# One decoder layer on one core: the samples' SSD states are read in the recurrent steps and updated in a second pass in the output steps

## The chip, the cores and the metric

The kernel runs on one core of one Trainium2 chip. The metric is the device time of one launch in microseconds. The engines are TensorE (PE, matmuls; PEld is its weight load), VectorE (DVE), ScalarE (ACT), GpSimd (POOL) and SyncE (SP). Each works through its own list of instructions in order and waits on semaphores that the others raise. ACT and SP also issue DMAs.

## What is computed

One layer of a hybrid decoder for one prompt of 256 tokens and 8 samples of one token each, D_MODEL 2048: a SwiGLU, a mixer with an RG-LRU group and a Mamba-2 SSD group side by side, a second SwiGLU, and a final norm. All is float32. What the change touches is the SSD recurrence of the 8 samples. With sequences of one token, the reference's scan comes to this for each sample and head (state 64 x 128):

```python
# ssd_scan with T = 1, for each sample b and head h
new_state = exp(dt * A) * old_state + outer(x * dt, B)   # stored as ssm_sample
y         = new_state @ C                                # + D * x, then gate and norm
# and so also
y         = exp(dt * A) * (old_state @ C) + (x * dt) * (B . C)
```

The last line is algebra, not a line of the reference. There are 16 heads in 2 groups; B and C (128 numbers) are those of the group. The state of all samples and heads is 4.2 MB, read once and written once.

## The kernel before, in words

PE's work is the weight matmuls. Weights come through SP's DMAs into `raw`, ACT copies each piece to `w_hi` (L686), rounded to the matmul's type, DVE makes `w_lo` = raw - w_hi (L1006), and PE multiplies hi x hi, lo x hi and hi x lo (L1648 to L1650). `w_hi` and `w_lo` have four buffers, so ACT may be three pieces ahead of PE. The program runs in steps of 8 pieces (24 matmuls a piece), each step in four slots j = 0 to 3; `u` = 4t + j counts slots of a kind of step. In every slot each engine does its part for two pieces and then its tasks (`act_tasks`, `dve_tasks`, `pe_tasks`), so the order on each engine is written out in the code.

Between the first SwiGLU and the second stand: 3 xbc steps and the dt step, 4 recurrent steps ("lru", u = 0 to 15), 2 z steps (u = 0 to 7), 4 output steps ("out", u = 0 to 15). The recurrent steps hold the RG-LRU with its convolutions (`conv_half`: L1205 twice, L1212, L1214 for each tile; the last one raises `conv_ready`) and its gate matmuls (`gates`, L1813 and L1814, which wait for `conv_ready`), the prompt's SSD products (`bcast`, `y_item`), and the samples' states.

The samples' states are 16 items of 128 x 512 (two heads' rows by four samples by 128 numbers). POOL does four tensor products or sums for each (`sample_item`): state times decay (L643), B times x dt (L647), their sum, which is the new state (L649), and new state times C (L652); DVE sums that over the 128 numbers (`sum_item`, L1287). B and C spread over the partitions come by `col_rows` on PE (8 matmuls into bank b7) and a copy by ACT (`spread_copy`, L817), one of each for every four items. ACT issues the load of each item (L806) and the store of its new state (L811) in the recurrent steps; four buffers `state` take turns.

In the last z slot (u = 7) DVE finishes `y_item` 15 (L1281, raises `y_placed` to 16), then the gate of the last two tiles (L1410 to L1419), the samples' y (L1424 to L1428, raises `sumsq_ready`), three w_lo, the reciprocal of the norm (L1433), and, tile by tile, L1436 and h_lo (L1440). PE has put `y_placed` and the sum over partitions (L1614, `sumsq_total`) after two pieces of the first output step. The output steps are weight pieces on PE, w_hi on ACT, and w_lo with `add_branch` (L1127 to L1138) on DVE. In slot 2 ACT copies the small output rows and issues eleven output DMAs (L924, L926). POOL has nothing after L661.

## Time and profile before

| | |
|---|---|
| median of 3 runs | 2179.3 us (2177.04 to 2180.01) |
| the profiled execution | 2176.04 us, span 2174.3 us |
| PE busy | 2119.3 us, 97% of the span |
| DVE busy | 1205.4 us, 55% |
| ACT busy | 859.6 us, 40% |
| POOL busy | 123.5 us, 6% |
| DMA | 534.17 MB, mean 246 GB/s |

Times in the trace count from the start of the span. The recurrent steps lie from about 1037 to 1180 us, the z steps to about 1230, the output steps to about 1327. A row of the timeline gives start, duration, engine, line, operation, what is written and read, and in brackets how long the engine was idle before, and who ended that. Two rows of one engine can overlap by some tenths of a microsecond, since an instruction starts while the one before it drains. Line numbers are those of the kernel before.

### The profile page before, as it was taken

Reading aid. Unit: us, or ns where it says so; the run is one execution under the profiler, and the core shown is the slowest. Engines: PE = TensorE matmul, PEld = TensorE weight load, DVE = VectorE, ACT = ScalarE, POOL = GpSimd, SP = SyncE. Lnnn points to the kernel's source line nnn. Section 1 sums busy time; section 2 is a strip of 40 time slices with the busy share of each in tenths; the row PEclk is TensorE's granted clock in tenths of the full one; section 3 lists DMA queues with packets and bytes.
Section 4 is the critical chain, followed back from the end, with each engine's and each line's share of the span. In section 5 each row is a group of like instructions: output and inputs, shape, how many; then the busy total and the mean of one; then the engine's idle time right before and its main releaser. Section 6 shows DMA issues by size and latency. Waiting matters only on the chain.

```text
span 2174.3 us, 40038 instructions
## 1 busy us (share of the span) xinstructions
PE 2119.3 (97%) x17437; PEld 1978.0 (91%) x17437; DVE 1205.4 (55%) x1649; ACT 859.6 (40%) x1058; POOL 123.5 (6%) x148
## 2 busy tenths in 40 slices
PE   6999999999999999999999999999999999999998
PEld 4988989988888889989988998999998999999998
DVE  4355576444444445577789967444444444445555
ACT  3433333333333333356655534333333333333332
POOL 0000000000000000011674000000000000000000
PEclk9999999999999999999999999999999999999999
DMA  9988886899888877647555485765667886755453
GB/s 357 344 300 293 286 279 245 279 337 367 304 307 309 308 277 258 239 147 222 161 172 161 156 281 205 263 236 173 228 235 254 306 277 237 248 169 171 146 175 117
DMA packets 394269, 534.17 MB, mean 246 GB/s; under 512 B 13031, under 2 KB 357999, under 8 KB 375407
## 3 DMA queue, kind: packets, MB, share of 16 engines
q1 hardware_dynamic: 371792, 519.28, 69.5%
q10 hardware_dynamic: 22303, 12.33, 2.0%
q8 instruction: 138, 2.26, 0.4%
q14 instruction: 36, 0.29, 0.0%
HBM read 524.37 MB, written 7.19 MB: 244 GB/s over the span
## 4 chain that ended last, share of the span: by engine, by line
PE 90%; DVE 6%; ACT 1%; issue 1%; SPq 1%; DMA 1%; ACTq 0%; DVEq 0%
PE main L1648 24%; PE main L1649 23%; PE main L1650 23%; PE b L1571 5%; PE main L1714 4%; PE main L1716 3%; PE main L1715 3%; DVE w_lo L1006 2%; PE b L1581 1%; ACT w_hi L686 1%; SPq L530 1%; PE b L1594 1%; DVE ntile L1099 1%; DMA first<-in_w_ada 1%; DVE h_lo L1104 1%
## 5 line engine op out<-in xcount | busy, mean ns | idle before, releaser
L1006 DVE TENSOR_TENSOR w_lo<-raw,w_hi 128x1024 fp32r<-128x1024 f32 (+2 forms) x720 | 791.3, 1106 | 868.3 <-ACT w_hi L686 866.9
L686 ACT ACTIVATE w_hi<-raw 128x1024 fp32r<-128x1024 f32 (+2 forms) x720 | 685.6, 956 | 1068.0 <-PE main L1650 908.5
L1648 PE MATMUL main<-h_hi,w_hi 128*128 128x264 f32 x2960 | 851.3, 288 | 11.6 <-DVE h_lo L1112 3.9
L1649 PE MATMUL main<-h_lo,w_hi 128*128 128x264 f32 x2960 | 843.6, 285 | 0.0
L1650 PE MATMUL main<-h_hi,w_lo 128*128 128x264 f32 x2960 | 842.3, 285 | 0.0
L1648 PEld LDWEIGHTS main<-h_hi,w_hi 128*128 128x128 f32 x2960 | 559.3, 189 | 31.8 <-DVE w_lo L1006 20.4
L1649 PEld LDWEIGHTS main<-h_lo,w_hi 128*128 128x128 f32 x2960 | 557.9, 188 | 0.4
L1650 PEld LDWEIGHTS main<-h_hi,w_lo 128*128 128x128 f32 x2960 | 557.7, 188 | 0.0
L1648 PE MATMUL main<-act_hi,w_hi 128*128 128x264 f32 x1408 | 402.1, 286 | 0.0
L1650 PE MATMUL main<-act_hi,w_lo 128*128 128x264 f32 x1408 | 400.4, 284 | 0.0
L1649 PE MATMUL main<-act_lo,w_hi 128*128 128x264 f32 x1408 | 399.8, 284 | 0.0
L1648 PEld LDWEIGHTS main<-act_hi,w_hi 128*128 128x128 f32 x1408 | 264.6, 188 | 10.1 <-issue 9.2
L1649 PEld LDWEIGHTS main<-act_lo,w_hi 128*128 128x128 f32 x1408 | 265.3, 188 | 0.0
L1650 PEld LDWEIGHTS main<-act_hi,w_lo 128*128 128x128 f32 x1408 | 264.6, 188 | 0.0
L1714 PE MATMUL main<-h_hi,w_hi 128*128 128x264 f32 x704 | 205.2, 292 | 9.1 <-DVE w_lo L1006 4.7
L1716 PE MATMUL main<-h_hi,w_lo 128*128 128x264 f32 x704 | 200.8, 285 | 0.0
L1715 PE MATMUL main<-h_lo,w_hi 128*128 128x264 f32 x704 | 200.8, 285 | 0.0
L1714 PEld LDWEIGHTS main<-h_hi,w_hi 128*128 128x128 f32 x704 | 133.8, 190 | 23.5 <-issue 18.6
L1715 PEld LDWEIGHTS main<-h_lo,w_hi 128*128 128x128 f32 x704 | 134.2, 191 | 0.0
L1716 PEld LDWEIGHTS main<-h_hi,w_lo 128*128 128x128 f32 x704 | 133.6, 190 | 0.0
L1571 PE MATMUL b<-ada,cT 128*32 128x512 f32 x1024 | 116.9, 595 | 0.0
L1571 PEld LDWEIGHTS b<-ada,cT 128*32 128x32 f32 x1024 | 29.8, 109 | 61.9 <-issue 57.6
(277 smaller groups left out, 1002.6 us busy)
## 6 DMA issues: line engine op xcount, KB each, us to landing
raw<-in_w_up SPq DMA_DIRECT2D x132, 1024.0 KB, 5.2
ada<-in_w_ada SPq DMA_DIRECT2D x112, 1024.0 KB, 8.6
raw<-in_w_down SPq DMA_DIRECT2D x96, 768.0 KB, 5.1
raw<-in_w_up SPq DMA_DIRECT2D x88, 512.0 KB, 5.3
raw<-in_w_in SPq DMA_DIRECT2D x36, 1024.0 KB, 5.4
ada<-in_w_ada_f SPq DMA_DIRECT2D x32, 1024.0 KB, 10.1
ada<-in_w_ada SPq DMA_DIRECT2D x56, 512.0 KB, 7.7
raw<-in_w_down SPq DMA_DIRECT2D x32, 512.0 KB, 4.3
```

Of the source, the lines that this page charges most:

```text
L530: sp.dma_start(quarter_slot(i)[:, v], quarter_columns(0, i, v)).then_inc((ada_landed, first_landed)[i // 4][i % 4], 16)
L686: A(split_view(w_hi, m, kind), raw_piece(m, kind), ACT.Copy).then_inc(hi_done, 1)
L1006: TT(split_view(w_lo, m, kind), raw_piece(m, kind), split_view(w_hi, m, kind).bitcast(F32), ALU.subtract).then_inc(lo_done, 1)
L1099: STT(ntile[:, k % 4, :], x[:, k, 0:NT], gain[:, k, 0:1], rstd[:, 0:NT], ALU.mult, ALU.mult).then_inc(aff_ready, 1)
L1104: return STT(h_lo[:, k, 0:NT], ntile[:, k % 4, :], mods[:, shift, k, 0:1], h_hi[:, k, 0:NT].bitcast(F32), ALU.add, ALU.subtract)
L1571: last = MM(b4[32 * j:32 * j + 32, :], cT[:, k, :], ada[:, k % 4, j * 512:(j + 1) * 512], start=k == 0, stop=k == KD - 1, tile_position=(0 ...
L1648: MM(out, wh, hi[:, k, :], start=k == 0, stop=False)
L1649: MM(out, wh, lo[:, k, :], start=False, stop=False)
L1650: last = MM(out, wl, hi[:, k, :], start=False, stop=k == total - 1)
L1714: MM(out, wh, h_hi[:, k, :], start=kk == 0, stop=False)
L1715: MM(out, wh, h_lo[:, k, :], start=False, stop=False)
L1716: last = MM(out, wl, h_hi[:, k, :], start=False, stop=kk == 3)
```

## The change

The states go through in two passes. In the recurrent steps POOL makes one product for each item, old state times C (`sample_read`), and DVE sums it as before; nothing is stored. In slot 1 of the z steps DVE multiplies the sums by the decay and adds x dt times (B . C); the products of B and C are made by DVE in recurrent slot 0 (`bc`) and summed over partitions by one matmul in z slot 0. In slot 3 of the z steps ACT loads the first four items a second time (`state_again`). POOL makes the new states (`sample_step`: state times decay, B times x dt, sum) after `y_placed` 16. ACT stores them and loads the other twelve items in output slots 1 to 12; each of these loads waits for the store from the same buffer. C is spread in recurrent slots j = 0 (four `col_rows` instead of eight there), B in z slots 1 to 4, into the space of `gates_w`, which is free by then; POOL's product of B goes to the space of `s0t`. The number of `col_rows` and copies stays eight.

```diff
-            def sample_item(n):
+            def sample_read(n):
...
-                ch.link(pool.tensor_tensor(st, st, dcs_f[:, t, bs].unsqueeze(2).to_broadcast([P, 4, NSTATE]), ALU.mult))
-                pool.wait_ge(spread_done, 2 * q + 1)
+                pool.wait_ge(spread_done, q + 1)
                 if n >= 2:
                     pool.wait_ge(st_sum, n - 1)
-                ch.link(pool.tensor_tensor(pr, spread_b[:, :, :],
+                pool.tensor_tensor(prod[n % 2], state[:, i, :, :], spread_c[:, :, :], ALU.mult).then_inc(st_prod, 1)
+
+            def sample_step(n):
+
+                (q, i), t, bs = (n // 4, n % 4), *item_place(n)
+                st, pr = state[:, i, :, :], outer[:, n % 2, :, :]
+                pool.wait_ge(st_in[i], 16 * (4 + q + 1))
+                ch.link(pool.tensor_tensor(st, st, dcs_f[:, t, bs].unsqueeze(2).to_broadcast([P, 4, NSTATE]), ALU.mult))
+                pool.wait_ge(spread_done, 4 + q + 1)
+                ch.link(pool.tensor_tensor(pr, spread_b[:, q, :, :],
                                            xsdt[:, t, bs].unsqueeze(2).to_broadcast([P, 4, NSTATE]), ALU.mult))
                 pool.tensor_tensor(st, st, pr, ALU.add).then_inc(st_new, 1)
...
             capture_h(3)
+            pool.wait_ge(y_placed, 16)
+            for n in range(16):
+                sample_step(n)
...
+            def state_again(n):
+
+                t, bs = item_place(n)
+                if n < 4:
+                    act.wait_ge(st_prod, 13 + n)
+                else:
                     act.wait_ge(st_out[n % 4], 16 * (n // 4))
...
                         state_load(r + 1)
-                    if 2 <= r <= 17:
-                        state_store(r - 2)
+                    if r == 19:
+                        for n in range(4):
+                            state_again(n)
...
-                if kind == "lru" and j < 2:
-                    spread_copy(2 * t + j, (spread_b, spread_c)[j][:, :, :])
+                if kind == "lru" and j == 0:
+                    spread_copy(t, spread_c[:, :, :])
+                if kind == "z" and 1 <= u <= 4:
+                    spread_copy(3 + u, spread_b[:, u - 1, :, :])
...
                 if kind == "out":
+                    for n in range(16):
+                        if u == 1 + 3 * n // 4:
+                            state_store(n)
+                    for n in range(4, 16):
+                        if u == 2 + 3 * (n - 4) // 4:
+                            state_again(n)
...
+                        TT(bc[:, :, :], xbc[:, 8:10, NT:COLS], xbc[:, 10:12, NT:COLS], ALU.mult).then_inc(bc_product, 1)
...
+                if kind == "z" and u == 1:
+                    dve.wait_ge(st_sum, 16)
+                    TT(samp[:, 0:KW, :], samp[:, 0:KW, :], dcs_f[:, :, :], ALU.mult)
+                    dve.wait_ge(bc_summed, 1)
+                    sums = b4[:, 0:2 * NB].rearrange("p (g b) -> p g b", g=2)
+                    for g in range(2):
+                        ins_ = TT(ybc[:, 4 * g:4 * g + 4, :], xsdt[:, 4 * g:4 * g + 4, :],
+                                  sums[:, g:g + 1, :].to_broadcast([P, 4, NB]), ALU.mult)
+                    ch.link(ins_)
+                    ch.link(TT(samp[:, 0:KW, :], samp[:, 0:KW, :], ybc[:, :, :], ALU.add))
...
+                if kind == "z" and u == 0:
+                    pe.wait_ge(bc_product, 1)
+                    pe.wait_ge(gate_taken, 16)
+                    MM(b4[:, 0:2 * NB], ones[:, :], bc[:, :, :].rearrange("p g b -> p (g b)"),
+                       start=True, stop=True).then_inc(bc_summed, 1)
+                if kind == "z" and 1 <= u <= 4:
+                    col_rows(3 + u)
```

How the order moves, at the two places that matter. First POOL, at items 14 and 15 of the recurrent steps and its end, before:

```order
L643 TENSOR_TENSOR state<-state,dcs_f 128x512
L647 TENSOR_TENSOR ntile<-spread_b,xsdt 128x512
L649 TENSOR_TENSOR state<-state,ntile 128x512
L652 TENSOR_TENSOR ntile<-state,spread_c 128x512
L643 TENSOR_TENSOR state<-state,dcs_f 128x512
L647 TENSOR_TENSOR part<-spread_b,xsdt 128x512
L649 TENSOR_TENSOR state<-state,part 128x512
L652 TENSOR_TENSOR part<-state,spread_c 128x512
L657 COPY outcol<-rec 128x2
L661 COPY outcol<-rec 128x2x8
```

And after (line numbers of the changed kernel; `ntile` and `part` are the two product buffers, `gates_w` now holds the spread B, `s0t` its product):

```order
L648 TENSOR_TENSOR ntile<-state,spread_c 128x512 [waits st_sum,spread_done,st_in2]
L648 TENSOR_TENSOR part<-state,spread_c 128x512 [waits st_sum,spread_done,st_in3]
L664 COPY outcol<-rec 128x2 [waits hl_ready]
L668 COPY outcol<-rec 128x2x8
L655 TENSOR_TENSOR state<-state,dcs_f 128x512 [waits st_in0,y_placed]
L657 TENSOR_TENSOR s0t<-gates_w,xsdt 128x512 [waits spread_done,pool_chain]
L659 TENSOR_TENSOR state<-state,s0t 128x512 [waits pool_chain]
L655 TENSOR_TENSOR state<-state,dcs_f 128x512 [waits st_in1]
L657 TENSOR_TENSOR s0t<-gates_w,xsdt 128x512 [waits spread_done,pool_chain]
L659 TENSOR_TENSOR state<-state,s0t 128x512 [waits pool_chain]
```

Six of eight products leave this place, and 48 of them stand behind `y_placed` 16, at the end of POOL's list. Second ACT's list, from the second norm's last tile to the first pieces of the second output step, before (L686 is w_hi, L912 the norm's h_hi; the output DMAs in the middle are the same in both, and end with `out_ssm_prompt`):

```order
L912 ACTIVATE h_hi<-xbc 128x264 [waits aff_ready]
L686 ACTIVATE w_hi<-raw 128x1024 [waits piece_used,w_landed0]
L918 ACTIVATE xdt<-b 128x512 [waits out_turned]
L919 ACTIVATE xdt<-b 128x128
L924 DMA out_lru_conv_prompt<-xdt 24x128 [waits out_rows_ready]
```

And after:

```order
L933 ACTIVATE h_hi<-xbc 128x264 [waits aff_ready]
L829 DMA out_ssm_sample<-state 128x4x128 [waits st_new] x2
L696 ACTIVATE w_hi<-raw 128x1024 [waits piece_used,w_landed0]
L829 DMA out_ssm_sample<-state 128x4x128 [waits st_new]
L824 DMA state<-in_state_ssm 128x4x128 [waits st_out0]
L824 DMA state<-in_state_ssm 128x4x128 [waits st_out1]
L945 ACTIVATE xdt<-b 128x512 [waits out_turned]
L946 ACTIVATE xdt<-b 128x128
L951 DMA out_lru_conv_prompt<-xdt 24x128 [waits out_rows_ready]
```

Three stores and two loads have come in, and the loads wait for stores issued just ahead of them (`st_out0`, `st_out1`).

## Rows read from the trace of the kernel before

**Rows 1.** The page: busy time, share of the span, instructions

```profile
PE 2119.3 (97%) x17437; PEld 1978.0 (91%) x17437; DVE 1205.4 (55%) x1649; ACT 859.6 (40%) x1058; POOL 123.5 (6%) x148
```

**Rows 2.** Stretches: length, busy time by engine, granted clock, DMA share, GB/s

```profile
core 0: us, PE busy (x) PEld busy (x) DVE busy (x) ACT busy (x) POOL busy (x), PEclk, DMA share, GB/s
1037.00:1180.00 143.00, 133.37 (x1037) 127.25 (x1036) 122.03 (x138) 83.48 (x128) 105.40 (x92) 0.98 0.55 166
...
1260.00:1327.00 67.00, 67.00 (x549) 67.00 (x548) 42.84 (x59) 24.39 (x23) 0.00 (x0) 1.00 0.75 256
```

**Rows 3.** Timeline of PE: every idle time in the recurrent steps

```profile
1089.78 0.78 PE L1813 MATMUL b<-cval,gates_w 128*128 128x264 f32 x1 [2.43 <-issue]
...
1125.72 0.68 PE L1813 MATMUL b<-cval,gates_w 128*128 128x264 f32 x2 [1.55 <-issue]
...
1135.39 0.68 PE L1813 MATMUL b<-cval,gates_w 128*128 128x264 f32 x2 [1.26 <-issue]
...
1160.58 0.68 PE L1813 MATMUL b<-cval,gates_w 128*128 128x264 f32 x2 [0.92 <-issue]
...
1169.33 0.68 PE L1765 MATMUL b<-tri,dA 128*128 128x128 f32 x4 [1.79 <-DVE s L1372]
...
1171.68 0.78 PE L1813 MATMUL b<-cval,gates_w 128*128 128x264 f32 x1 [1.68 <-issue]
```

**Rows 4.** Timeline of DVE ahead of the first idle time, POOL working

```profile
1084.62 2.50 DVE L1205 SCALAR_TENSOR_TENSOR cfull<-cin,small,cfull 128x288 f32<-128x288 f32 x2
1087.16 1.37 DVE L1212 SCALAR_TENSOR_TENSOR cval<-cin,small,cfull 128x256 f32<-128x256 f32 x1
1088.46 1.23 DVE L1214 SCALAR_TENSOR_TENSOR cval<-cin,small,cfull 128x8 f32<-128x8 f32 x1
```

**Rows 5.** Timeline of DVE, the same instructions a slot later, POOL idle

```profile
1093.68 1.13 DVE L1205 SCALAR_TENSOR_TENSOR cfull<-cin,small,cfull 128x288 f32<-128x288 f32 x2
1094.84 0.49 DVE L1212 SCALAR_TENSOR_TENSOR cval<-cin,small,cfull 128x256 f32<-128x256 f32 x1
1095.24 0.23 DVE L1214 SCALAR_TENSOR_TENSOR cval<-cin,small,cfull 128x8 f32<-128x8 f32 x1
```

**Rows 6.** Timeline of POOL beside rows 4, one item's first three products

```profile
1084.37 1.23 POOL L643 TENSOR_TENSOR state<-state,dcs_f 128x512 f32<-128x512 f32 x1
1085.68 1.14 POOL L647 TENSOR_TENSOR part<-spread_b,xsdt 128x512 f32<-128x512 f32 x1
1086.89 1.36 POOL L649 TENSOR_TENSOR state<-state,part 128x512 f32<-128x512 f32 x1
```

**Rows 7.** DVE: two w_lo beside POOL; L1281's duration min/median/max in ns

```profile
1161.64 3.99 DVE L1006 TENSOR_TENSOR w_lo<-raw,w_hi 128x1024 fp32r<-128x1024 f32 x2
...
L1281 DVE SCALAR_TENSOR_TENSOR xbc<-xbc,dfeat,b x16: 334/339/348, 1083.2 to 1231.1; 128x128 f32<-128x128 f32 x16
```

**Rows 8.** Timeline of DVE in the last z slot, up to the w_lo

```profile
1232.20 0.68 DVE L1416 SCALAR_TENSOR_TENSOR xbc<-xbc,silu_g 128x512 f32<-128x512 f32 x1
...
1234.37 0.22 DVE L1424 TENSOR_TENSOR xbc<-xbc,dfeat 128x64 f32<-128x64 f32 x1
...
1235.61 3.48 DVE L1006 TENSOR_TENSOR w_lo<-raw,w_hi 128x1024 fp32r<-128x1024 f32 x3
```

**Rows 9.** Timeline of PE in the output steps

```profile
1236.11 0.60 PE L1614 MATMUL b<-sumsq,ones 128*128 128x264 f32 x2
...
1250.45 0.39 PE L1648 MATMUL main<-h_hi,w_hi 128*128 128x264 f32 x1 [0.93 <-DVE h_lo L1440]
...
1260.04 0.28 PE L1648 MATMUL main<-h_hi,w_hi 128*128 128x264 f32 x1
```

**Rows 10.** Timeline of ACT around the output DMAs

```profile
1249.01 1.04 ACT L686 ACTIVATE w_hi<-raw 128x1024 fp32r<-128x1024 f32 x1
...
1255.81 2.01 ACT L686 ACTIVATE w_hi<-raw 128x1024 fp32r<-128x1024 f32 x2 [5.11 <-issue]
```

**Rows 11.** The stores of new states: ns to issue, us to landing

```profile
L811 ACTq DMA_DIRECT2D out_ssm_sample<-state x16: 378/520/893, 1050.3 to 1185.6; - x16
...
DMA to landing us min/median/max: 2.3/4.2/5.8
```

**Rows 12.** Timeline of DVE, the w_lo behind the output DMAs

```profile
1256.97 1.23 DVE L1006 TENSOR_TENSOR w_lo<-raw,w_hi 128x1024 fp32r<-128x1024 f32 x1 [2.20 <-ACT w_hi L686]
```

More of the change, by code:

```diff
@@ L210, in build @@
             ("shift_row", [P, D], F32), ("yrows", [P, 2, D], F32), ("ysrow", [P, P], F32)])
-        (xbc, out_l, cin, cfull, cval, xdt, xdec, btok, cbm, s0, s0t, state, spread_b, spread_c,
+        (xbc, out_l, cin, cfull, cval, xdt, xdec, btok, cbm, s0, s0t, state, spread_c,
          gates_w, th, rec, dA, spt, sp2, sp3, sp4, lam2, half_b, exp_a, cst, decl, tot, cdf, dfeat,
-         dts_f, dcs_f, xsdt, zs, later, ncs) = layout([
+         dts_f, dcs_f, xsdt, zs, later, ncs, bc, ybc) = layout([
             ("xbc", [P, KX, COLS], F32),
@@ L229, in build @@
             ("dts_f", [P, KW, NB], F32), ("dcs_f", [P, KW, NB], F32), ("xsdt", [P, KW, NB], F32),
-            ("zs", [P, KW, NB], F32), ("later", [P, P], F32), ("ncs", [P, NHEAD], F32)])
+            ("zs", [P, KW, NB], F32), ("later", [P, P], F32), ("ncs", [P, NHEAD], F32), ("bc", [P, 2, NB], F32), ("ybc", [P, KW, NB], F32)])
         prod_even = (ntile[:, 2:4, :].rearrange("p a n -> p (a n)")
@@ L234, in build @@
         gel, aa = silu_g, part
+        spread_b = gates_w.rearrange("p a t n -> p (a t n)").rearrange("p (q b n) -> p q b n", q=4, b=4)
+        outer = s0t.rearrange("p (a b n) -> p a b n", a=2, b=4)
         dtq = part2[:, 0, :]
@@ L283, in build @@
         st_new, st_prod, st_sum = sem("st_new"), sem("st_prod"), sem("st_sum")
+        bc_product, bc_summed = sem("bc_product"), sem("bc_summed")
         z_tanh, sz_ready = sem("z_tanh"), sem("sz_ready")
@@ L664, in _ @@
             for n in range(16):
-                sample_item(n)
+                sample_read(n)
                 if n % 4 == 1:
@@ L814, in spread_copy @@
                 act.wait_ge(col_spread, n + 1)
-                if n >= 2:
-                    act.wait_ge(st_prod, 4 * (n // 2))
+                if 1 <= n < 4:
+                    act.wait_ge(st_prod, 4 * n)
                 A(dst.rearrange("p b n -> p (b n)"), b7[:, :], ACT.Copy).then_inc(spread_done, 1)
@@ L1786, in col_rows @@
             def col_rows(n):
-                q, cc = n // 2, n % 2
+                is_b, q = n // 4, n % 4
                 g, half = q // 2, q % 2
@@ L1793, in col_rows @@
                     pe.wait_ge(spread_done, n)
-                if n % 2 == 0 and n:
-                    pe.wait_ge(gate_taken, 2 * n)
+                    pe.wait_ge(gate_taken, 16 if is_b else 4 * n)
                 for i in range(4):
                     col = NT + 4 * half + i
-                    last = MM(b7[:, i * P:(i + 1) * P], xbc[:, 8 + 2 * cc + g, col:col + 1].to_broadcast([P, P]),
+                    last = MM(b7[:, i * P:(i + 1) * P], xbc[:, (8 if is_b else 10) + g, col:col + 1].to_broadcast([P, P]),
                               ident[:, :], start=True, stop=True)
@@ L1807, in gates @@
                 if t % 2 == 0:
-                    pe.wait_ge(spread_done, t + 2)
+                    pe.wait_ge(spread_done, t // 2 + 1)
                 if t == 0:
@@ L1854, in pe_tasks @@
                 if kind == "lru":
-                    if j < 2:
-                        col_rows(2 * t + j)
-                    else:
+                    if j == 0:
+                        col_rows(t)
+                    if j >= 2:
                         gates(2 * t + j - 2)
+                if kind == "z" and u == 0:
[5 more added lines that the diff above has]
+                    col_rows(3 + u)
                 if kind == "out" and u == 1:
```

9 lines of the change are left out of this document (3 added, 6 removed).

## Prediction, written before the changed kernel ran

> **What bounds the kernel now.** First the page's busy shares: TensorE (PE) is busy 97% of the span [rows 1], so a change pays only where it removes idle PE time, or adds it. Then the stretches: in the recurrent steps (1037 to 1180 us) PE is busy 133.37 of 143 us, while VectorE (DVE) is busy 122.03 and GpSimd (POOL) 105.40; in the output steps from 1260 on PE is busy without a gap and DVE 42.84 of 67 us [rows 2]. Third, PE's idle times inside the recurrent steps: 2.43, 1.55, 1.26, 0.92, 1.79 and 1.68 us, **9.63 us** in all [rows 3]. Five stand before L1813, the gate matmul, which waits for `conv_ready`. The trace calls the releaser "issue", but DVE's L1214, whose end raises `conv_ready`, runs from 1088.46 for 1.23 us and so ends at 1089.69 [rows 4], and PE starts at 1089.78 [rows 3]. The sixth (1169.33) waits for DVE's work on `s0`. So DVE is late there, and PE waits for it.
>
> Why is DVE late? The same instructions stand twice in its rows. With POOL idle, L1205 (two of them) takes 1.13 us, L1212 0.49, L1214 0.23 [rows 5]; ten microseconds earlier, with POOL's products running end to end [rows 6], 2.50, 1.37 and 1.23 [rows 4]. That is 0.69, 0.88 and 1.00 us more for each instruction, 3.25 us in four of them; w_lo (L1006) took 3.99 us for two where 1.23 is its free time [rows 7, 12], 0.77 us more each. Each of these reads two tensors in SBUF. L1281, which has one operand in PSUM, never took over 0.35 us in 16 instructions [rows 7]. DVE loses **0.7 to 1.0 us to each POOL product that meets such an instruction**, and three products last from 1084.37 to 1088.25, 3.9 us a sample item [rows 6].
>
> This is what the Trainium skill says (SBUF — State Buffer, "Who interferes with whom"): a DVE instruction with two SBUF inputs contends with a GpSimd instruction that reads SBUF. By that rule, the trace agrees in kind; its stronger half comes below as a rival.
>
> **The change, part by part.**
>
> 1. *Recurrent steps, less POOL work.* Each of 16 items goes from four products to one, so 48 of 64 go. Before the first stall the four contended instructions alone lost 3.25 us, more than the 2.43 us that PE waited [rows 3 to 5]; with one product an item a hit or so of 0.7 to 1.0 us remains, and L1006 and the scans further up lose less too. The waits for POOL's sums and ACT's waits for new states go as well. What is late next would be ACT's convolution start, which I see no sign of. PE's clock belongs here: the granted mean is 0.98 over 143 us [rows 2], about 2.9 us lost to stretches at the lower level (1.2 instead of 2.4 GHz), which come with the longer idle times (L1813 takes 0.78 us at 1089.78 and at 1171.68, 0.68 as a pair elsewhere [rows 3]). Bounds: each of the six idle times shrinks by one missed hit of 0.7 us, 4 us; and all goes, 9.63 + 2.9 = 12.5. I take **-12.0**, near the upper end, because the stretch (3.25 us in four instructions) exceeds every single idle time.
>
> 2. *Moved column rows and the B.C product.* Four `col_rows` with their copies go from the recurrent to the z steps: as many matmuls as before, zero net. One small matmul and some six small DVE products are new; L1424, as wide, takes 0.22 us [rows 8]. In the z steps DVE gains the time of the moved matmuls, and POOL is silent. Taken at zero; uncovered 1.3 us.
>
> 3. *The first four items of the second pass meet the second norm.* POOL now waits for `y_placed` 16, the end of DVE's L1281 in the last z slot, and its states have been loaded. From there DVE makes the chain that PE waits for: gate, squares, sample sum, then w_lo, reciprocal, and the eight parts of h. There is no slack in it: `sumsq` is done when L1006 starts at 1235.61 and PE asks for it at 1236.11, and the last h_lo already costs 0.93 us at 1250.45 [rows 8, 9]. POOL's 12 products need 12 x 1.3 = 16 us [rows 6], the same stretch. DVE has ten instructions with two SBUF inputs in its first 8 us: three like L1416 (0.8 each, between L1205's 0.69 and L1212's 0.88), four like L1424 (1.00 each, L1214's loss), three w_lo (0.8): 2.4 + 4.0 + 2.4 = **+8.8**. Bounds: half the products meet nothing, 5; all twelve cost 0.9, 11.
>
> 4. *Stores and loads on ACT's queue.* Ahead of its w_hi for the second piece of the second output step ACT now issues three stores and two loads, and each load waits for the store of its buffer to land. A store takes 0.52 us to issue and lands after 4.2 (2.3 to 5.8) [rows 11]. The second load cannot go before 0.52 + 4.2 = 4.7 us, plus about 0.4 for its issue, 5.1, of which 1.04 is the w_hi that stood there before [rows 10]: 4.1 us more. Before, w_hi started at 1255.81 (after the output DMAs), its w_lo ended at 1256.97 + 1.23 = 1258.20, and PE took that piece at 1260.04 [rows 9, 10, 12]: 1.84 us of cover. So 2.3 us, and 0.4 for a product that may meet the w_lo: **+2.7** (0.5 to 5). Queued behind these waits are only ACT's own w_hi; later ones have three pieces of lead.
>
> 5. *The other twelve items in the output steps.* 36 products; if each met a DVE instruction at 0.8 us, 28.8 us more for DVE, which is idle 67 - 42.84 = 24.2 us there [rows 2], some 21 of them while POOL runs: 8 us short. If only every second one does, 14.4, it fits. The lead is zero at the start (part 4), so lumps count; I take **+4.0** (0 to 8).
>
> 6. *Clock.* PE idles for over 5 us at once in part 3. One stretch at the lower level costs half of the 2.9 us of two: **+1.4** (0 to 3).
>
> Not priced: 4.2 MB read a second time, since the output steps move 256 GB/s [rows 2], and the page's first slice 357.
>
> Sum: -12.0 + 8.8 + 2.7 + 4.0 + 1.4 = **+4.9 us**. The profiled run took 2176.04 us (span 2174.3), the median of the runs is 2179.3, 3.3 above; the profiled one would become 2180.9, and on the median I forecast 2184.2.
>
> **The rivals.**
>
> *Faster: POOL gives way.* POOL's products in the second pass could be the ones that wait, and DVE's chain loses only 4 us; w_lo is served in time (+1), no clock stretch: -12 + 4 + 1 = -7, 2172. For it: only 12 products lie on the chain. Against: in rows 4 and 6 POOL kept 1.14 to 1.36 us a product while DVE's small instruction took five times its time. It decides if L1424 to L1427's successors take under 0.5 us.
>
> *Much slower: the output steps do not fit both engines.* If a product shuts DVE out for all of its 1.14 to 1.36 us, 36 of them hold some 45 us. Beside them stand at least the w_lo, one for each of the 549 / 24 = 23 pieces in the 67 us, 28 us, and at most all of DVE's 43 [rows 2]: 6 to 21 us too many for 67, say 14 instead of 4. Then -12 + 8.8 + 2.7 + 14 + 1.4 = +15, 2194. Against it: L1205 grew by 0.69 us only, beside products of 1.14 and more [rows 4 to 6], so they overlap in part. The Trainium skill (SBUF — State Buffer, the same section) has this rule: whoever issues first holds the port for the whole instruction and the other fully blocks.
>
> *The stalls stay.* The change may not free PE in the recurrent steps, because the single products still hit the convolutions or ACT is next: gain 4 instead of 12, so +13, 2192. For it: DVE is at 85% there [rows 2]. Against: it would have to be late without most of its losses.
>
> **How the numbers follow.** Forecast 45% (its own range 2178 to 2191), POOL gives way 20%, does not fit 12%, stalls stay 13%, and 10% for mixtures on either side. The range takes in the first rival and nearly the second: 2170 to 2198. A measurement of this kernel tells about 0.2%, 4.4 us, from no change. Faster by more: the first rival and a few of the mixtures, 24%. Slower by more: the two slow rivals and 26 points of the forecast's 45, which lies just over the line, 51%. Within: 25%.
>
> **What would show it.** Right if L1813's idle times are gone, and if PE instead waits over 5 us for the `sumsq` matmul of the first output step, behind DVE instructions of 0.2 us stretched to over 1 us; then 2 to 3 us at the second piece of the next step, behind w_lo; then small waits for w_lo while POOL works. Wrong if PE meets the norm without waiting (faster), if the waits for w_lo add up to more than 8 us (much slower), or if L1813 still waits (stalls stay). The forecast itself falls if the new waits of the output steps sum to under 8 or over 25 us.

## The result, and the profile after

The changed kernel takes 2182.65 us (median of 20 runs, 2179.69 to 2186.46), the kernel before 2177.78 us (20 runs, 2175.93 to 2180.07). The ratio is 1.0022 with a 95% interval of 1.0016 to 1.0028: **4.9 us slower**, and slower beyond doubt, though only just above the 0.2% line of the prediction. The profiled execution has a span of 2180.9 us where the one before had 2174.3.

Four stretches of the changed kernel, in the columns of [rows 2] (length, busy time of PE, of its weight loads, of DVE, ACT and POOL, granted clock, DMA share, GB/s): the recurrent steps, the z steps, the norm, and most of the output steps.

```profile
1024.00:1167.00 143.00, 143.00 (x1147) 137.75 (x1146) 107.07 (x165) 93.54 (x139) 48.92 (x50) 1.00 0.49 155
1167.00:1219.00 52.00, 51.24 (x438) 48.86 (x437) 46.31 (x88) 31.19 (x50) 0.33 (x2) 1.00 0.53 163
1218.00:1250.00 32.00, 25.19 (x178) 23.94 (x179) 30.80 (x42) 11.61 (x19) 17.20 (x12) 0.89 0.47 144
1250.00:1318.00 68.00, 61.31 (x481) 60.25 (x479) 54.11 (x50) 20.25 (x20) 58.24 (x36) 0.97 0.96 313
```

In the recurrent steps PE now works all 143 us at a clock of 1.00; before it was 133.37 of 143 at 0.98 [rows 2]. All six idle times of [rows 3] are gone. The price stands in the last two lines, where before PE had only the two short waits for h_lo ahead of 1260 and none behind it [rows 2, 9]. PE's own timeline names each new wait in its last bracket (start, duration, line, then the idle time ahead of it and what ended it):

```profile
1228.88 1.22 PE L1652 MATMUL b<-sumsq,ones 128*128 128x264 f32 x2 [4.89 <-DVE sumsq L1466]
...
1246.18 0.39 PE L1686 MATMUL main<-h_hi,w_hi 128*128 128x264 f32 x1 [0.91 <-DVE h_lo L1478]
...
1257.59 0.39 PE L1686 MATMUL main<-h_hi,w_hi 128*128 128x264 f32 x1 [1.68 <-DVE w_lo L1033]
...
1265.84 0.39 PE L1686 MATMUL main<-h_hi,w_hi 128*128 128x264 f32 x1 [2.11 <-DVE w_lo L1033]
...
1295.81 0.39 PE L1686 MATMUL main<-h_hi,w_hi 128*128 128x264 f32 x1 [0.31 <-DVE w_lo L1033]
...
1304.32 0.39 PE L1686 MATMUL main<-h_hi,w_hi 128*128 128x264 f32 x1 [2.38 <-DVE w_lo L1033]
...
1319.64 0.39 PE L1686 MATMUL main<-h_hi,w_hi 128*128 128x264 f32 x1 [1.84 <-DVE w_lo L1033]
```

L1652 is the `sumsq` matmul of [rows 9], L1686 the main matmul there. The 0.91 us for h_lo was there before (0.93), and two shorter ones ahead of it, 0.18 and 0.83 us, stand where 0.56 stood. The rest is new: 4.89 us at the norm, 1.68 at the second piece of the second output step, and then 2.11, 0.31, 2.38 and 1.84, together **6.64 us**, for w_lo. The timeline of DVE shows what stands behind the 4.89 us, the successors of [rows 8]:

```profile
1222.33 1.67 DVE L1457 TENSOR_TENSOR sumsq<-sumsq,part 128x512 f32<-128x512 f32 x1
1224.03 0.94 DVE L1462 TENSOR_TENSOR xbc<-xbc,dfeat 128x64 f32<-128x64 f32 x1
1225.01 1.08 DVE L1463 TENSOR_TENSOR xbc<-xbc,samp 128x64 f32<-128x64 f32 x1
1226.13 1.30 DVE L1464 SCALAR_TENSOR_TENSOR xbc<-xbc,zs 128x64 f32<-128x64 f32 x1
1227.47 0.96 DVE L1465 TENSOR_TENSOR samp<-xbc 128x64 f32<-128x64 f32 x1
1228.46 0.27 DVE L1466 TENSOR_REDUCE sumsq<-samp 128x8 f32<-128x64 f32 x1
1228.65 6.09 DVE L1033 TENSOR_TENSOR w_lo<-raw,w_hi 128x1024 fp32r<-128x1024 f32 x3
```

Four products of 64 columns, 0.22 us before, take 0.94 to 1.30 us. Three w_lo take 6.09 us where they took 3.48 [rows 8]. L1466, which reads one tensor, keeps 0.27 us. POOL's timeline beside the four small products shows how the two engines share:

```profile
1223.40 1.50 POOL L655 TENSOR_TENSOR state<-state,dcs_f 128x512 f32<-128x512 f32 x1
1224.97 1.04 POOL L657 TENSOR_TENSOR s0t<-gates_w,xsdt 128x512 f32<-128x512 f32 x1
1226.09 1.26 POOL L659 TENSOR_TENSOR state<-state,s0t 128x512 f32<-128x512 f32 x1
1227.31 1.04 POOL L655 TENSOR_TENSOR state<-state,dcs_f 128x512 f32<-128x512 f32 x1
```

They take turns, a whole instruction at a time. POOL's products end at 1224.90, 1226.01, 1227.35 and 1228.35, and each of DVE's four small ones ends 0.07 to 0.08 us later: it has waited for nearly the whole product. The long ones do the same. In the second pass 21 w_lo are lengthened, and every one of them ends 1.08 us after a POOL product has ended, where a w_lo that meets nothing takes 1.22; POOL's products beside w_lo end 0.90 us (L655, L657) or 1.13 to 1.15 (L659) after the w_lo has ended, where they take 1.04 and 1.26 when they meet nothing. So all but 0.11 to 0.14 us of an instruction stands behind the whole of the other engine's. The one that comes first keeps its time: L1454 starts at 1220.17 and takes 0.68 us as before the change [rows 8], and POOL's product that starts at 1220.30 takes 1.45.

In the output steps four w_lo in a row take 8.14 us, 2.03 each, and POOL's products, in turns with them, as much as 2.15:

```profile
1263.84 8.14 DVE L1033 TENSOR_TENSOR w_lo<-raw,w_hi 128x1024 fp32r<-128x1024 f32 x4
```

```profile
1264.79 2.15 POOL L659 TENSOR_TENSOR state<-state,s0t 128x512 f32<-128x512 f32 x1
1266.90 2.02 POOL L655 TENSOR_TENSOR state<-state,dcs_f 128x512 f32<-128x512 f32 x1
1269.00 1.90 POOL L657 TENSOR_TENSOR s0t<-gates_w,xsdt 128x512 f32<-128x512 f32 x1
1270.97 2.15 POOL L659 TENSOR_TENSOR state<-state,s0t 128x512 f32<-128x512 f32 x1
```

An item then takes 6.2 us (L659 to L659), where the stores stand four in three slots of two pieces, a piece being 2.93 us of PE: one each 4.4 us. ACT's timeline, with the instructions that issue transfers as ACTq, shows what follows. L829 is the store of new states, L696 w_hi:

```profile
1277.96 1.06 ACT L696 ACTIVATE w_hi<-raw 128x1024 fp32r<-128x1024 f32 x1 [1.87 <-PE main L1688]
1278.54 6.58 ACTq L829 DMA_DIRECT2D out_ssm_sample<-state  x2
1285.16 0.52 ACTq L824 DMA_DIRECT2D state<-in_state_ssm  x1
1285.78 2.01 ACT L696 ACTIVATE w_hi<-raw 128x1024 fp32r<-128x1024 f32 x2 [6.75 <-issue]
```

Two stores hold ACT for 6.58 us instead of about 1, because the new state they store isn't made; ACT is idle for 6.75 us before the w_hi behind them, and DVE's w_lo comes after that. This stand by itself costs PE little: DVE is idle for 0.73 us, and PE's next wait is 0.31 us, ten microseconds on. But in the second pass ACT is idle for 3 to 8 us between two w_hi seven times, DVE is idle for w_hi 3.93 and 3.31 us more, and then makes w_lo of 2 us each. The waits of 2.38 and 1.84 us come after some 10 us in which DVE was never idle. The queue and the lengthened w_lo make them together.

Where the time went, read by following one instruction of each place through both traces: the last z slot's y item starts 12.28 us earlier than before; the last h_lo, 18.84 us behind it before, is now 26.92 us behind (+8.08); the second piece of the second output step is then 2.45 us early (1257.59 against 1260.04), so another +1.8; the first norm wait of the feed-forward steps behind is 6.75 us late, so +9.2 from there on.

### The profile page after: what moved, and what is told of

Its sections match the earlier page's. It is cut to its first block, busy times and chain, and to the rows that moved or that the text cites. A ratio compares the mean times of both kernels' runs of the same rounds, so it can differ in the third digit from the quotient of the medians.

```text
span 2180.9 us, 40054 instructions
## 1 busy us (share of the span) xinstructions
PE 2123.3 (97%) x17439; PEld 1982.3 (91%) x17439; DVE 1208.4 (55%) x1654; ACT 858.8 (39%) x1058; POOL 139.0 (6%) x148
## 4 chain that ended last, share of the span: by engine, by line
PE 84%; DVE 6%; POOL 3%; issue 3%; ACT 1%; DMA 1%; SPq 1%; ACTq 0%; DVEq 0%; POOLq 0%
PE main L1686 22%; PE main L1687 22%; PE main L1688 22%; PE b L1609 5%; PE main L1752 4%; PE main L1754 3%; PE main L1753 3%; DVE w_lo L1033 2%; POOL state L659 1%; PE b L1619 1%; POOL state L655 1%; POOL s0t L657 1%; ACT w_hi L696 1%; SPq L533 1%; PE b L1632 1%
## 5 line engine op out<-in xcount | busy, mean ns | idle before, releaser
L1033 DVE TENSOR_TENSOR w_lo<-raw,w_hi 128x1024 fp32r<-128x1024 f32 (+2 forms) x720 | 805.9, 1128 | 874.0 <-ACT w_hi L696 872.7
L696 ACT ACTIVATE w_hi<-raw 128x1024 fp32r<-128x1024 f32 (+2 forms) x720 | 684.6, 956 | 1078.4 <-PE main L1688 887.7
L1686 PE MATMUL main<-h_hi,w_hi 128*128 128x264 f32 x2960 | 853.8, 288 | 19.3 <-DVE w_lo L1033 11.6
L1686 PEld LDWEIGHTS main<-h_hi,w_hi 128*128 128x128 f32 x2960 | 562.3, 190 | 40.3 <-DVE w_lo L1033 30.9
L1686 PE MATMUL main<-act_hi,w_hi 128*128 128x264 f32 x1408 | 402.1, 286 | 0.0
L1686 PEld LDWEIGHTS main<-act_hi,w_hi 128*128 128x128 f32 x1408 | 264.7, 188 | 10.1 <-issue 9.2
```

Of the source, the lines that this page charges most:

```text
L696: A(split_view(w_hi, m, kind), raw_piece(m, kind), ACT.Copy).then_inc(hi_done, 1)
L1033: TT(split_view(w_lo, m, kind), raw_piece(m, kind), split_view(w_hi, m, kind).bitcast(F32), ALU.subtract).then_inc(lo_done, 1)
L1686: MM(out, wh, hi[:, k, :], start=k == 0, stop=False)
```

## The experiments

All ratios are against the kernel before, run beside each experiment on the same chip; 0.001 is 2.2 us. The intervals reach 0.0009 to 0.0016 to either side, so two experiments that lie less than about 0.0015 apart are not told from each other. Line numbers in rows are those of each kernel.

**The first term alone.** The kernel before, with three of an item's four products taken out: the new states are left out, the old ones are stored.

```
-  ch.link(pool.tensor_tensor(st, st, dcs_f[...], ALU.mult))
...
-  ch.link(pool.tensor_tensor(pr, spread_b[...], xsdt[...], ALU.mult))
-  pool.tensor_tensor(st, st, pr, ALU.add).then_inc(st_new, 1)
+  pool.memset(pr[:, 0, 0:1], 0.0).then_inc(st_new, 1)
```

> The kernel before, with three of the four products of each sample item taken out (they are one memset of a single column, so the new states are left out and the old ones are stored); the recurrent steps keep their loads, stores and waits, nothing is added behind them. It measures the first term of the sum by itself. Theory (POOL's products that read SBUF are what makes DVE late): the six idle times of PE before L1813 and the state update go, 9.6 us and some 2 to 3 us of clock, so 11 to 13 us below before, 2164 to 2166 us. Rival (the gain came from the queues and waits that the change took out of the recurrent steps, not from the products): those are all still there, so at most 4 us below, 2172 or more.

Measured: 2164.44 us, ratio 0.9940 (0.9926 to 0.9953), 13.1 us less. The stretch of the recurrent steps has no idle PE time:

```profile
1024.00:1167.00 143.00, 143.00 (x1150) 137.91 (x1151) 108.89 (x164) 93.00 (x140) 44.60 (x66) 1.00 0.59 181
```

The rival falls: stores, loads and waits are all still there. The gain is that DVE meets fewer products: 13.1 us, where the trace of the change has 12.28.

**The change without its second products.** The states are loaded a second time, waited for and stored; the 48 products are left out, and so are the new states.

```
+  pool.memset(pr[:, 0, 0:1], 0.0).then_inc(st_new, 1)
+  pool.wait_ge(st_new, n + 1)
+  return
```

> The changed kernel with all 48 second-pass products left out (one column is written instead, so new states are left out); the second loads, the stores and all waits between them stay. This prices what the DMAs and their waits on ACT's queue cost alone. Theory A: the loss in norm and output steps (some 19 us in the traces) was nearly all products; what stays is the wait of 1 to 2 us at the second piece of the second output step, so 2182.7 - 17 = 2164 to 2168 us. Rival D (the second load of 4.2 MB and ACT's queue are the cost): at least 6 us of the output steps' loss stays, 2171 us or more.

Measured: 2165.58 us, ratio 0.9948 (0.9932 to 0.9963). That is 16 us under the change. It is 1.7 us above the last experiment by the ratios, which is within the noise of the two (nothing to some 6 us): that is what the second reading, the moved matmuls and the extra issues on ACT's queue cost together. Nearly all that the change loses comes with the products of the second pass.

**Products that only write.** The 48 products replaced by as many memsets of 1344 columns; the new states are left out.

```
+  fill = gates_w.rearrange("p a t n -> p (a t n)")[:, 0:1344]
+  ch.link(pool.memset(fill, 0.0))
+  ch.link(pool.memset(fill, 0.0))
+  pool.memset(fill, 0.0).then_inc(st_new, 1)
```

> The changed kernel, but each of the 48 second-pass products is replaced by a POOL memset of 1344 columns, about 1.2 us long, that reads nothing; the new states are left out. POOL is as busy as before, or nearly. Theory A in its narrow form (a DVE instruction with two SBUF inputs is held up by POOL instructions that READ SBUF): no DVE instruction is stretched, no wait at the sumsq matmul, no w_lo waits beyond the one that stands behind ACT's DMA issues; 2165 to 2170 us. Rival C (any POOL work of that length holds DVE up, or what costs is POOL being busy so that ACT waits for its stores): DVE stretched as before, 2178 to 2183 us. If only ACT's waits matter, items are done in 3.6 us and the time lies between.

Measured: 2173.76 us, ratio 0.9982 (0.9973 to 0.9991), between what the two theories had, which the expectation names as the third outcome. POOL's timeline and DVE's at the place of the four small products:

```profile
1222.19 1.22 POOL L658 MEMSET gates_w<- 128x1344 f32 x1
1223.47 1.23 POOL L659 MEMSET gates_w<- 128x1344 f32 x1
1224.76 1.22 POOL L657 MEMSET gates_w<- 128x1344 f32 x1
1226.03 1.22 POOL L658 MEMSET gates_w<- 128x1344 f32 x1
```

```profile
1223.76 0.23 DVE L1469 TENSOR_TENSOR xbc<-xbc,dfeat 128x64 f32<-128x64 f32 x1
1224.02 0.23 DVE L1470 TENSOR_TENSOR xbc<-xbc,samp 128x64 f32<-128x64 f32 x1
...
1225.00 3.48 DVE L1040 TENSOR_TENSOR w_lo<-raw,w_hi 128x1024 fp32r<-128x1024 f32 x3
```

POOL works end to end there, and DVE's products keep 0.23 us and its three w_lo 3.48, as before the change. So it isn't POOL's being busy that costs: it is POOL's *reading* from SBUF while DVE reads two tensors there. The kernel is still some 7 us slower than the one without products. Its PE waits for w_lo, 0.99, 2.50 and 0.80 us, come after DVE was idle for w_hi (5.19, 7.29 and 2.72 us), while its w_lo kept 1.22 us, so ACT's waits in the stores and loads cost by themselves. Here POOL was late because the states were: a load issued at 1259.14 us landed 16.1 us later.

**Only the first four items left out.** These are the ones that meet the norm; their new states are left out.

```
+  if n < 4:
+      pool.wait_ge(spread_done, 4 + q + 1)
+      pool.memset(pr[:, 0, 0:1], 0.0).then_inc(st_new, 1)
+      pool.wait_ge(st_new, n + 1)
+      return
```

> The changed kernel, but for the first four items of the second pass POOL makes one write of one column instead of its three products, so the new states of these four items are left out; loads, stores and all waits stay. Theory A: the norm chain on DVE returns to its 18.8 us from 26.9, PE's wait before the sumsq matmul goes, time 2182.7 - 8 = 2174 to 2176 us. Rival B (chain late for another reason): wait of 4.9 us stays, time within 2 us of 2182.7.

Measured: 2175.70 us, ratio 0.9992 (0.9983 to 1.0001), 6.5 us under the change. PE meets `sumsq` without waiting, and the waits for h_lo are those of the kernel before:

```profile
1237.81 0.39 PE L1691 MATMUL main<-h_hi,w_hi 128*128 128x264 f32 x1 [0.57 <-DVE h_lo L1483]
1240.48 0.39 PE L1691 MATMUL main<-h_hi,w_hi 128*128 128x264 f32 x1 [0.93 <-DVE h_lo L1483]
```

Behind them the waits for w_lo are 1.75, 0.61, 0.62, 2.39, 0.79 and 2.13 us, 8.3 us, as in the change (8.3 with its 1.68). The norm term of the sum, 8.1 us in the trace, comes back: 6.5 us, which the noise does not tell from 8.1.

**The second pass after the norm.** Everything is computed; POOL starts when the last h_lo is made, and stores and loads stand two slots later.

```
-  pool.wait_ge(y_placed, 16)
+  pool.wait_ge(h_ready, 3 * KD)
...
-  if u == 1 + 3 * n // 4:            # stores
+  if u == 3 + 3 * n // 4:
...
-  if u == 2 + 3 * (n - 4) // 4:      # loads
+  if u == 4 + 3 * (n - 4) // 4:
```

> The changed kernel, whole, but POOL starts the second pass only when the last h_lo of the second norm is made (it waits for h_ready instead of y_placed), and ACT's stores and later loads come two slots later. Theory A (POOL's products stretch DVE's two-input instructions wherever they meet): PE's 4.9 us wait before the sumsq matmul goes, and the 8 us by which DVE's norm chain was longer with it; the w_lo wait of 1.7 us at the second piece of the second output step goes too. The 48 products then share 12 slots with w_lo instead of 36, so the waits for w_lo in the output steps stay or grow by 1 to 3 us. Time 8 to 10 us below the changed kernel's 2182.7, some 2173 to 2176, that is 0 to 2 % of a percent range around -0.1 to -0.2 % against the kernel before. Rival B (the norm chain is late for another reason, for example the DVE work moved into the z steps): the 4.9 us wait stays and the time is within 2 us of the changed kernel's.

Measured: 2180.48 us, ratio 1.0012 (1.0003 to 1.0021). The norm is free again, but the time did not come back: a miss. The 2.2 us under the change are within the noise. The stretch from 1250 to 1335 us and the group of main matmuls from 1250 to 1330, with its idle time on the right:

```profile
1250.00:1335.00 85.00, 73.86 (x550) 71.02 (x550) 67.88 (x62) 23.94 (x24) 65.35 (x41) 0.94 0.89 288
```

```profile
L1686 PE MATMUL main<-h_hi,w_hi 128*128 128x264 f32 x175 | 52.2, 298 | 11.0 <-DVE w_lo L1033 11.0
```

11.0 us of waits for w_lo instead of 8.3 (6.64 and 1.68), and a clock of 0.94. 48 products at up to 2 us each, with items that wait for their loads, fill what is left of the output steps, and two stores again hold ACT for 4.9 to 5.5 us. Moving the products off the norm trades one wait for another.

**Eight buffers.** The second four lie in `th` and `xdec`, which are free by then, so that no load waits for a store just issued. The stores stand a slot later. The loads move the other way: items 4 to 7 are loaded ahead of the row DMAs, and the second eight two slots earlier than in the change.

```
+  more = [v[:, 0:1024]... for v in (th..., xdec)]
...
-  act.wait_ge(st_out[n % 4], 16 * (n // 4))
+  if count:
+      act.wait_ge(gone, count)       # only from item 8 on
```

> The whole change with eight buffers for the states of the second pass instead of four (the second four lie in buffers of the recurrence that are free by then), so that no load waits for a store that has just been issued, and the stores stand a slot later. The same 48 products start at the same time, beside the second norm. If ACT's blocking in the stores and loads is what makes w_hi and so w_lo late in the output steps (theory: some 4 to 5 of the 6.6 us of waits there), this is 4 to 6 us below the change, 2176 to 2179 us, and the waits for w_lo there sum to under 2.5 us. If contention of POOL and DVE makes w_lo late by itself (rival), the sum of the waits stays at 5 us or more and the time within 2 us of the change's 2182. The waits of the norm (4.9 us before the sumsq matmul) stay in both.

Measured: 2181.41 us, ratio 1.0014 (1.0005 to 1.0023). The waits for w_lo did fall as that theory has it:

```profile
L1712 PE MATMUL main<-h_hi,w_hi 128*128 128x264 f32 x193 | 55.4, 287 | 3.3 <-DVE w_lo L1058 2.6 <-DVE h_lo L1503 0.7
```

2.6 us in the 75 us from 1250 on, a little over the 2.5 of the theory; the changed kernel has 8.3 there. The median w_lo takes 2.00 us there, against 2.06, so lengthened w_lo alone do not make those waits: with w_hi on time most of them are covered. How much of the 5.7 us is ACT's queue stays open, since POOL also has 30 products left in this stretch instead of 36. And the time fell by 1.7 us only, which is within the noise. The stretch of the norm shows why:

```profile
1218.00:1250.00 32.00, 23.19 (x150) 21.80 (x150) 31.34 (x33) 10.37 (x17) 24.47 (x18) 0.84 0.32 99
```

POOL has 24.47 us of work there instead of 17.20. In the changed kernel it paused for items 4 and 5, whose buffers were not free, and that pause spared the eight parts of h. Without it PE waits 0.75, 1.56, 1.61 and 0.66 us for h_lo, 4.6 us where the change has 0.83 and 0.91, and the clock falls to 0.84. The gain went into a new wait.

**Eight buffers and the late start.** Both edits together, stores and loads one slot later again.

> The same eight buffers, and POOL starts the second pass only when the second norm has been made (as in e1_late), with stores and loads a slot later again. POOL then has some 89 us for 16 items of 4.3 (free) to 6 us (beside DVE). Theory (ACT's blocking is the larger part of the waits in the output steps, contention the smaller): the norm costs nothing and the waits sum to under 4 us: 2169 to 2173 us. Rival (contention alone makes w_lo late, because 48 products are packed more tightly): no better than e1_late, 2178 to 2181.

Measured: 2175.59 us, ratio 0.9995 (0.9986 to 1.0004). Better than either edit alone (1.0012 and 1.0014), and under 2178 as the rival would not have it, but not the 2169 to 2173 of the theory. The waits for w_lo sum to 7.5 us: POOL's items take 6 us, the stores are due each 4.4, and ACT still stood 4.57, 5.73 and 5.71 us in pairs of stores. With 48 products behind the norm POOL is busy 68.3 of the 75 us from 1250 to 1325, and the stores catch up with it.

**A third of the products to ACT.** As the last one, and ACT multiplies the old states by the decays. POOL has two products an item. The stores and the later loads also stand one slot earlier than in the last one, so the two edits are not told apart here.

```
+  for b in range(4):
+      ins_ = A(buf[:, b, :], buf[:, b, :], ACT.Copy, scale=dcs_f[:, t, at:at + 1])
+  ins_.then_inc(st_scaled, 1)
```

> As e9_eight_late, and ACT multiplies the old states by their decays (four activations of 128 columns an item, some 1.1 us) in POOL's place, so that POOL has 32 products instead of 48, 2.7 us an item free and 4 us beside DVE. ACT is idle for over 40 of the 68 us of the output steps. Theory: POOL keeps ahead of the stores, ACT never blocks, fewer w_lo meet a product: 2166 to 2170 us, faster than the kernel before (2176.5). Rival (ACT's queue becomes the bound, because 1.1 us more stand before its w_hi): waits for w_lo of over 5 us in the output steps, 2173 or more.

Measured: 2173.99 us, ratio 0.9984 (0.9975 to 0.9993). The ratio is 0.0011 below the last one's, within the noise, and both theories hold in part: the waits for w_lo sum to 6.3 us. PE's timeline has one large wait:

```profile
1254.06 0.59 PE L1728 MATMUL main<-h_hi,w_hi 128*128 128x264 f32 x1 [5.04 <-DVE w_lo L1074]
```

It stands behind an ACT queue with 16 activations of scaling, a store that waited 1.96 us for its state, and the row DMAs, all ahead of the w_hi at 1251.33.

**The same, later entries.** Stores one slot later, behind the row DMAs; loads and scalings of the second eight items two. Item 4 is scaled in the z steps, 5 to 7 in output slots 0, 1 and 3.

```
-  if u == 2 + 3 * n // 4:            # stores
+  if u == 3 + 3 * n // 4:
...
-  if u == 3 + 3 * (n - 8) // 4:      # loads
+  if u == 5 + 3 * (n - 8) // 4:
```

> As e7_act_scales, but each of ACT's queue entries a slot or two later: stores one slot later (none before the output rows' DMAs any more), loads and scalings of the second eight items two slots later, and the scalings of items 4 to 7 spread over four slots. In e7_act_scales PE waited 5.04 us once, for a w_lo behind a w_hi that stood behind ACT's wait for POOL's second new state (1.96 us), 13 scalings and the rows' DMAs; a later 0.95 us had the same kind of cause. Theory (all that is left is ACT's queue): these waits go, the clock stays up, 2173.99 less 5 to 6: 2167 to 2170 us, ratio 0.995 to 0.997. Rival (w_lo is late by contention even where ACT is on time): waits of w_lo of 3 us or more stay, 2172 to 2174.

Measured: 2172.04 us, ratio 0.9974 (0.9962 to 0.9985). Faster than the kernel before, a little short of what was expected. Its stores stand in the same slots as those of eight buffers with the late start (0.9995), and its later loads one slot behind, so this pair shows what the scaling on ACT is worth: 0.0021, 4.6 us. Two waits remain, 1.37 and 2.61 us, just behind the row DMAs.

**POOL one step later still.** POOL starts when PE has used the fifth piece of the first output step. The stores and the loads and scalings of the second eight stand one slot later with it; items 4 and 5 are scaled in the z steps, 6 and 7 in output slots 3 and 4.

```
-  pool.wait_ge(h_ready, 3 * KD)
+  pool.wait_ge(piece_used, 8 * S_OUT + 5)
```

> As e10_later_stores, but POOL starts the second pass one step of PE's work later, when PE has used the fifth piece of the first output step, after ACT's row DMAs; stores and the second eight loads and scalings are one slot later with it, and the scalings of items 4 and 5 are made in the z steps. In e10_later_stores PE still waited 1.37 and 2.61 us for w_lo just behind the row DMAs, with w_lo of 1.7 to 2.1 us beside POOL. Theory (that is the one place with no lead, and contention is free elsewhere): those waits go or fall under 1 us, 2168 to 2171 us, ratio 0.995 to 0.997. Rival (the waits only move on to where POOL now starts): no gain over e10_later_stores, 0.9974 or more, with waits of 3 us or more further on.

Measured: 2176.22 us, ratio 0.9991 (0.9982 to 1.0000): a miss, and the edit did not do what it was meant to. PE comes to that piece before the norm is done, because the step's first pieces multiply the other half of h. POOL started at 1239.66 us, in the middle of the norm, and PE paid for it:

```profile
1242.69 0.41 PE L1728 MATMUL main<-h_hi,w_hi 128*128 128x264 f32 x1 [2.38 <-DVE h_lo L1519]
1245.30 0.59 PE L1728 MATMUL main<-h_hi,w_hi 128*128 128x264 f32 x1 [1.09 <-DVE h_lo L1519]
1248.68 0.59 PE L1728 MATMUL main<-h_hi,w_hi 128*128 128x264 f32 x1 [1.70 <-DVE h_lo L1519]
```

It says nothing about the lead at the row DMAs, but repeats what the norm costs: 5.2 us of waits for h_lo against 1.5, from six POOL products that started before the last h_lo. The ratio is 0.0017 worse than the last one's, and 0.0033 worse than that of the next, which scales the first eight items in the same slots and has POOL's start behind the norm.

**Scalings out of the way of the row DMAs.** POOL starts at the end of the norm again; item 5 is scaled in the z steps, 6 and 7 behind the row DMAs.

> As e10_later_stores (POOL starts at the end of the second norm again; in e11_after_rows the count of used pieces was reached at 1239.66 us, while the norm still ran to 1248, since that step's first pieces need the other half of h, so POOL met the norm and its waits grew to 5.2 us). Only the scalings of items 5 to 7 are moved: 5 into the z steps, 6 and 7 behind the row DMAs, so that 2.5 us of scaling and 0.94 us of waiting for a load no longer stand ahead of ACT's w_hi at the start of the output steps. Theory (lead at the row DMAs is what is short): the waits of 1.37 and 2.61 us go or halve, 2167 to 2171 us, ratio 0.995 to 0.997. Rival (w_lo beside POOL is late there by itself): ratio 0.9974 or more with the same two waits.

Measured: 2168.47 us (5 runs, 2167.74 to 2170.93), ratio **0.9958** (0.9944 to 0.9971), 9 us under the kernel before and 14 under the change, with everything computed. The step from 0.9974 lies within the noise; the step from 0.9995 does not. The waits are 0.29 us for `sumsq`, 0.53 and 0.91 for h_lo, as before the change, and 0.25 and 2.27 for w_lo; of the whole group from 1250 to 1330:

```profile
L1728 PE MATMUL main<-h_hi,w_hi 128*128 128x264 f32 x184 | 53.3, 290 | 2.5 <-DVE w_lo L1074 2.5
```

The wait of 1.37 us fell to 0.25, that of 2.61 only to 2.27: the first was ACT's lead. The second has w_hi in time and w_lo of over 2 us beside POOL, so there the rival holds.

## Why the prediction was right

It gave 2184.2 us with 2170 to 2198; measured 2182.65, slower by 4.9 where it said 4.9. Part of that is luck. The two profiled executions lie 6.6 us apart, more than the medians, and the terms read from them sum to 6.8 (-12.3 + 8.1 + 1.8 + 9.2): one term was well short, and three others were each a little better than priced.

- *Bound and cause.* DVE late by POOL's products: shown, by taking out products alone (0.9940). "The stalls stay" falls.
- *Part 1, -12.0.* 12.28 us at the last z slot in the profile, 12.75 over the recurrent and z steps, since the start of the stretch was 0.47 us later; 13.1 by the experiment. The reasoning that the stretch exceeds each idle time, and that the clock comes back, held.
- *Part 2, 0.* One new wait of 0.76 us at 1168.26, for a w_lo. Within its bound of 1.3.
- *Part 3, +8.8.* 8.08 us. The form was right (products of 0.22 us at 0.94 to 1.30, three w_lo at 2.03), and so "POOL gives way" falls for this place: it was to be seen by these small products at under 0.5 us. The extra time of those four is 3.4 us, of the w_lo 2.6, of the two 512-column squares 1.7 (L1456 and L1457, 1.41 and 1.67 us for 0.69 each), while L1454, the third that was priced, lost nothing; the priced 4.0, 2.4 and 2.4 are close.
- *Part 4, +2.7.* 1.8 us. Counted from PE's last wait for h_lo, w_hi started 5.36 us later before (1250.45, 1255.81) [rows 9, 10] and 8.42 us now (1246.18, 1254.60): 3.1 us, where 4.1 were priced. The first two stores went out at 1243.90, ahead of the last h_hi, and had partly landed; the loads' wait that is left is 1.63 us of ACT's time.
- *Parts 5 and 6, +4.0 and +1.4.* **This is the term that was mis-sized.** 9.2 us from the second output step on, against at most 5.4: 6.64 us of waits and, with a clock of 0.97 over 68 us, 2 us of clock; 0.6 us is not placed. Two things were missing. POOL's products were priced at their free duration, so an item was to take 4 us; but the two engines take turns, so POOL's products wait for w_lo too, up to 2.15 us each, and an item takes 6. And part 4 stopped at the first stores: "later ones have three pieces of lead". With items of 6 us the later stores wait for `st_new` by 5 to 6 us, time and again. Three pieces are 8.8 us, so one such wait would be covered; but the next comes before w_lo of 2 us each have won the lead back (DVE is never idle in the 10 us ahead of the waits of 2.38 and 1.84). The eight buffers, with w_lo as long, had 2.6 us of waits for 8.3, so w_lo's length alone is not the cause; how the rest divides between queue and turns stays open.
- *The rival "does not fit"* priced the extra at 14 instead of 4. The truth, 9.2, is about half way, and by the prediction's own mark of 8 us for waits of w_lo (8.3 with the 1.68) it was nearer than its 12% said. Its mechanism, that a product shuts DVE out for its whole length, is the one that the rows show. The prediction argued against it with L1205, which grew by 0.69 us only beside products of 1.14 and more: but both L1205 end 0.3 us after a product's end [rows 4, 6], and the free duration is 0.56, so what they gained was a start while the product was under way. What the rival left out is that POOL is shut out in turn. That spreads the 36 products over most of the stretch, and DVE still has 14 us idle in 68.
- *The signs.* L1813's idle times are gone. The wait for `sumsq` was 4.89 us where "over 5" was named, the one at the second piece 1.68 where "2 to 3" was, each just short. The waits for w_lo came to 8.3 us, a sign of the much slower rival, but its 2194 us did not come. The new waits of the output steps sum to some 13.6 us, inside 8 to 25.

The Trainium skill (SBUF — State Buffer, "Who interferes with whom") has the pair of engines and operands right: reading POOL against DVE with two SBUF inputs. The memsets, which read nothing, left DVE's products and w_lo alone. The same section calls what the two share an exclusive lock, and writes that whoever issues first holds it for the whole instruction, though that sentence stands there under VectorE's 2-port modes and not under two SBUF inputs. By that rule, the trace agrees here too: 21 of 21 lengthened w_lo end 1.08 us after a POOL product's end, and w_lo of 1.22 us beside products of 1.04 come to about 2.03 each, in turns. That both engines grow is no sign of a lower rate.

## What to carry to other kernels

Work taken off a contended stretch has to land where the engines it contends with have slack *and* where no chain without slack runs beside it; the norm behind the z steps had none, and 12 of the 48 products cost 8 us there, where taking all 48 away saved 12 elsewhere. Price both sides of a contention, and look at where instructions end: when two engines take turns, a short instruction waits for a whole long one, the mover's own items take longer too, and every queue that waits for them (here ACT's, with w_hi behind the stores) inherits it. A transfer that waits for another engine belongs in a queue late enough never to wait: of the 14 us between the change and the best version, more buffers and the later start gave 6 together and, alone, about 2 each, within the noise; a third of the products given to an engine that does not contend, with its queue entries well placed, gave the other 8.

## What the hardware showed unexpectedly

- POOL and DVE take turns by whole instructions: a DVE product of 0.22 us beside POOL's products takes 0.94 to 1.30 us and ends 0.07 to 0.08 us after one of them; a w_lo ends 1.08 us after one, in 21 cases of 21.
- POOL instructions that only write don't hold up DVE's products and w_lo: 0.23 us and 3 w_lo in 3.48 us beside memsets of 1.22 us end to end. A copy of 16 columns was the exception: 0.50 us beside products, 0.66 beside memsets, where 0.17 is its time before the change. Both times it ended 0.03 us after POOL's instruction, so it waited for a memset too.
- ACT works on the states beside DVE at no visible cost: in the z steps of the best version 24 such activations of 128 columns (0.39 us each) ran, and DVE's w_lo took 1.22 us as in the change.
- A pause of POOL that looked like lost time, 20.9 us of waiting for loads in the changed kernel, protected the norm; removing its cause made the waits for h_lo 2.7 us longer.
- A store of a new state lands after up to 11.1 us in the output steps, a load after up to 12.8, where the stores took 5.8 at most in the recurrent steps before [rows 11]; the output steps move 313 GB/s instead of 256 [rows 2]. That the one makes the other is not shown.
